# Latent heads in 64 plain and 32 turned rows, a mask laid out beforehand, and eight gate tiles moved into the MLP

## The chip, the core and the metric

The kernel runs on one core of one Trainium2 chip. The metric is the device time of one execution in microseconds, lower is better. A core has five engines with queues of their own: TensorE (PE in the profile; PEld is its weight loads), VectorE (DVE), ScalarE (ACT), GpSimd (POOL) and SyncE (SP), which here only issues transfers. They meet in semaphores.

## What is computed

Two transformer blocks run one after the other on 256 tokens of width 1024, in float32. The first has two layers (a window and neighbourhood attention beside 256 context tokens, then a differential attention), each with an MLP of width 4096. The second has two layers that mix a latent attention (6 heads), a dilated attention (6 heads) and a sparse one (4 heads). What the change touches is this:

```python
# first block: shifts, scales and gates of every layer come from small vectors
mx = jax.nn.silu(c) @ ada_w[i] + ada_b[i]            # 6 x 1024 columns, for x and for ctx
...
s_nb = einsum(q, kb) * scale + bias                  # neighbourhood: bias from b_rpb
s_nb = jnp.where(mask, s_nb, -jnp.inf)               # 16 of the columns of a grid row
...
hx = hx + gx2 * _mlp(...)                            # gx2: the last gate
# second block, latent attention
qa = heads(cq @ w_uq[l], 6)                          # a head: 64 plain + 32 turned
qa_rope = apply_rope(qa[..., 64:], cos, sin)
ka_nope = heads(ckv @ w_uk[l], 6)                    # 64 a head
ka_rope = apply_rope(p_kr, cos, sin)                 # 32, shared by all heads
s = (qa_nope . ka_nope + qa_rope . ka_rope) * 96 ** -0.5   # causal
```

## The kernel before

Feature rows lie on the 128 partitions, tokens in the columns. All weights come as a stream of 286 units of 128 x 1024 float32 (`wall`) through a ring of four slots `raw`. ACT rounds a unit to its high half `whi` (`split_hi`, line 501), DVE subtracts and gets the low half `wlo` (`split_lo`, line 768), and PE multiplies high with high, high with low and low with high (`mm3`, lines 1351 to 1353). Both halves are made three units ahead (`ahead`). A unit gives 128 output features: 24 matmuls, of 512 columns in the first block's first layer, of 256 later. `project`, `values`, `project_out` and `mlp` on PE run over the units. The first three units of each are interleaved (`TOGETHER`).

**Gate tiles.** The adaptive parameters are computed on the side. 144 tiles of 128 x 1024 (`aall`) come through a second ring of four, `aring`. The first 16 are used by PE at the start, eight by PE inside the first attention (`ada_tile`), and the others by DVE as dot products of a row with a broadcast vector: `ada_dot` (line 795) for the first layer's tiles, `ada_dots` (line 826) inside the first MLP. A tile of kind "d" takes two dots (x and context), "s" and "b" one. Where they are used is written out by hand: `ADA_L0` says how many tiles follow each of the 12 steps of the first projection and the 8 steps of the first output projection (`ada_tiles`), `ADA_STEPS` which kinds follow each of the 16 steps of an MLP quarter, four quarters. Biases are added behind (`ada_bias` line 810, `ada_sums` line 838). SP issues weights and tiles in one queue in that same order (`mlp_loads`), each behind a wait that its slot is free.

**Start and first attention.** `project(p_l0)` makes ten query and key units, rotated (`rope`, lines 927 to 930, on DVE; its cosine product on POOL, line 1295), and two value units. POOL adds a column mask from `cst` to the position bias `BI` in two instructions (line 1305, semaphore `rpb_done`), on which DVE waits before the attention. `attend` exists on PE, ACT, DVE and POOL. A job is two heads over up to 256 queries; its scores (line 1484), bias and maxima (952 to 959), exponentials (613), transposes (1501), values (1532), normalisation (1018) and split are spread over seven steps of a software pipeline. PE begins it after `a_used` says that the tiles before it are done. The output projection's results are added to X by DVE (line 1064); squares of ACT are summed by POOL (1234) and PE (1398) for the next norm.

**First MLP.** `mlp` on DVE does in step j: `split_lo` of unit j + 3, then the step's dots, then for j < 8 the square of the ReLU (line 1083) and the low half of the hidden tile (line 1073), for j >= 8 the gated addition to X (line 1064). PE's unit 8 contracts over all eight hidden tiles and waits before its k-th group for the k-th low half (semaphore `hid`). The whole is a loop of four quarters on every engine. The last gate (columns 40 to 47 of `ada`), which the additions use, is computed before the MLP.

**Latent attention, twice.** The query of a head has its own unit, six units (`p_uq`, six k-steps each): rows 0 to 63 plain, 64 to 95 turned. Each is rotated over 96 rows, with a cosine of one on the first 64. ACT copies `w_uk`'s results in six pieces to `KA` (lines 737, 738); POOL copies the turned key, which came in the ninth unit of `p_a` beside the index key, into all six heads (line 1322, `kr_done`), adds the selection to `AL` (line 1326) and only then makes the rotations' cosines. ACT copies the index key twice into `KI`. A score matmul contracts over 96 rows. In `attend` POOL widens the reciprocals (line 1249), then multiplies the row by the gate (line 1256), for which DVE's line 1018 waits, and makes low halves (line 1260).

Of the kernel before, what the change touches and what calls it, by code (L numbers as in the profile page):

```python
# [26 lines left out]
F32 = mybir.dt.float32  # L27
# [25 lines left out]
C_WIN, C_NBR, C_CAU = 1280, 1792, 2304  # L53
C_END = 2688
# [19 lines left out]
B2_UNITS = B2_FM1 + B2_FM2 + 6 + KT + 6 + 1 + 1 + KT  # L74
# [21 lines left out]
def program(nc, wall, aall, const, prm, xin, rpb, ali, out):  # L96
    with ExitStack() as top:
# [85 lines left out]
        QA = sb("QA", [P, 6, N], F32, b2)  # L183
        KA = sb("KA", [P, 6, N], F32, b2)
        VA = sb("VA", [P, 2, 384], F32, b2)
        KK = sb("KK", [P, N], F32, b2)
        KI = sb("KI", [P, N], F32, b2)
# [109 lines left out]

        p_l0 = Proj(U_L0, [l0_tile(i) for i in range(L0_FM)])
# [15 lines left out]
        for l in range(2):  # L314
            u = U_B2 + l * B2_UNITS
            p_a.append(Proj(u, [Tile(256, None, PQ[:, i, :]) for i in range(8)] + [Tile(256, "m", KK[0:96, :])]))
# [7 lines left out]
            p_uq.append(Proj(u + 37, [Tile(256, "m", QA[0:96, i, :], None, 96 ** -0.5) for i in range(6)]))  # L324
# [5 lines left out]
        class Job:  # L330
# [3 lines left out]
            def __init__(self, q, k, parts, bias, v, dst, b0=0, sink=None, diff=False, gate=None, tile=None):  # L334
# [4 lines left out]

        def two(ap, n):  # L340
            return ap[:, None, :].to_broadcast([P, 2, n])

# [74 lines left out]
        def _(sp):  # L417
# [14 lines left out]
            def mlp_loads(u0, ada=False):  # L432
                with sp.Fori(0, QUARTERS) as it:
# [61 lines left out]
        def _(act):  # L495
# [44 lines left out]
            def evac(pr, i):  # L540
# [7 lines left out]
                n = 128 if t.rope == "q" else 96  # L548
                if r >= 2:
                    act.wait_ge(sem("rope_out"), r - 1)  # L550
                ins = act.activation(wk1[0:n, r % 2, 0:N], bank[0:n, 0:N], ACT.Copy, scale=t.scale)
                if t.rest is not None:
                    ins = act.activation(t.rest, bank[:, N:2 * N], ACT.Copy, scale=t.scale)
# [134 lines left out]
            for l in range(2):  # L688
# [41 lines left out]
                for i in range(6):  # L730
# [12 lines left out]
                out_proj(u0 + 45, norms[f"ln{l}"])  # L743
# [1126 lines left out]
```

## Time and profile before

| | |
|---|---|
| runs, median of 3 | 1475.39 us (1473.77 to 1479.74) |
| the profiled execution | 1478.54 us, its span 1476.7 us |
| mean granted clock of TensorE | 0.947 |
| busy: PE, PEld | 1359.0 us (92%), 1177.8 us (80%) |
| busy: DVE, ACT, POOL | 1039.2 us (70%), 643.8 us (44%), 225.9 us (15%) |
| read from memory | 233.90 MB, 159 GB/s over the span |

The span runs from the first to the last instruction. Busy times add up an engine's instructions; a matmul's end is modelled and overlaps the next one's start, so a busy PE is not one at its peak. PE's matmul of 512 columns is shown with 0.39 to 0.40 us and starts about every 0.23 us at full clock. An idle time belongs to the wait that ended it.

### The profile page before, as it was taken

The numbers are of one execution on the slowest core, as the hardware profiler recorded it, in microseconds if no ns is written. First come the engines' busy times: TensorE is split into PE (matmuls) and PEld (weight loads), VectorE is DVE, ScalarE is ACT, GpSimd is POOL, SyncE is SP. The second block draws the span as 40 slices with busy tenths as digits, with TensorE's granted clock in tenths as the row PEclk, the third lists the DMA queues.
The fourth block names the chain that finished last, engine by engine and source line by source line (L and its number), as shares of the span: only waits on it lengthen the run. The fifth ranks groups of instructions, "written<-read, shape, count | busy, mean of one in ns | idle before, by whom it ended". The sixth has DMA issues, their size and how long they took to land. (4 is left out here: it accounts for less than half of the span.)

```text
span 1476.7 us, 24608 instructions
## 1 busy us (share of the span) xinstructions
PE 1359.0 (92%) x9014; PEld 1177.8 (80%) x9014; DVE 1039.2 (70%) x1803; ACT 643.8 (44%) x1287; POOL 225.9 (15%) x294
## 2 busy tenths in 40 slices
PE   6898999499999999979999999999999978899977
PEld 4576678388888888868896789999899967899857
DVE  0698867889697796988416675766664975755964
ACT  2424761242231423325226654455455465455563
POOL 2030221100000000012102710000210126010324
PEclk7898999699999999989999999999999989899988
DMA  7954124357578575744220155665465533445511
GB/s 279 274 172 156 55 62 143 128 185 268 188 243 284 194 264 179 253 175 143 87 90 25 30 157 171 213 185 185 132 222 171 162 96 107 144 144 170 173 42 44
DMA packets 67799, 236.14 MB, mean 160 GB/s; under 512 B 7296, under 2 KB 12416, under 8 KB 67456
## 3 DMA queue, kind: packets, MB, share of 16 engines
q1 hardware_dynamic: 67712, 234.98, 48.7%
q8 instruction: 54, 0.88, 0.2%
q14 instruction: 33, 0.27, 0.1%
HBM read 233.90 MB, written 1.05 MB: 159 GB/s over the span
## 5 line engine op out<-in xcount | busy, mean ns | idle before, releaser
L768 DVE TENSOR_TENSOR wlo<-raw,whi 128x1024 fp32r<-128x1024 f32 x286 | 361.8, 1267 | 176.4 <-ACT whi L501 171.9
L501 ACT ACTIVATE whi<-raw 128x1024 fp32r<-128x1024 f32 x286 | 301.6, 1055 | 244.3 <-PE ps L1353 232.4
L1351 PE MATMUL ps<-Hh,whi 128*128 128x512 f32 (+1 forms) x848 | 297.2, 351 | 17.3 <-DVE Hl L885 14.2
L1352 PE MATMUL ps<-Hl,whi 128*128 128x512 f32 (+1 forms) x848 | 295.1, 348 | 0.0
L1353 PE MATMUL ps<-Hh,wlo 128*128 128x512 f32 (+1 forms) x848 | 295.0, 348 | 0.0
L1351 PEld LDWEIGHTS ps<-Hh,whi 128*128 128x128 f32 x848 | 162.9, 192 | 41.7 <-issue 14.8
L1351 PE MATMUL ps<-Gh,whi 128*128 128x256 f32 x624 | 180.5, 289 | 4.5 <-DVE Gl L885 3.8
L1352 PEld LDWEIGHTS ps<-Hl,whi 128*128 128x128 f32 x848 | 163.1, 192 | 21.4
L1353 PEld LDWEIGHTS ps<-Hh,wlo 128*128 128x128 f32 x848 | 162.7, 192 | 21.8
L1352 PE MATMUL ps<-Gl,whi 128*128 128x256 f32 x624 | 179.0, 287 | 0.0
L1353 PE MATMUL ps<-Gh,wlo 128*128 128x256 f32 x624 | 178.7, 286 | 0.0
L1352 PE MATMUL ps<-HIDl,whi 128*128 128x512 f32 (+1 forms) x512 | 173.2, 338 | 0.0
L1353 PE MATMUL ps<-HIDh,wlo 128*128 128x512 f32 (+1 forms) x512 | 173.2, 338 | 0.0
L1351 PE MATMUL ps<-HIDh,whi 128*128 128x512 f32 (+1 forms) x512 | 173.2, 338 | 0.0
L826 DVE CUSTOM_DVE_ANT_0 ps<-aring,SB 128x1024 f32<-128x1024 f32 x112 | 144.3, 1288 | 3.8 <-DVE AC L826 2.6
L1351 PEld LDWEIGHTS ps<-Gh,whi 128*128 128x128 f32 x624 | 121.8, 195 | 5.9 <-issue 4.7
L1352 PEld LDWEIGHTS ps<-Gl,whi 128*128 128x128 f32 x624 | 121.8, 195 | 0.0
L1353 PEld LDWEIGHTS ps<-Gh,wlo 128*128 128x128 f32 x624 | 121.7, 195 | 0.0
L1351 PEld LDWEIGHTS ps<-HIDh,whi 128*128 128x128 f32 x512 | 96.3, 188 | 11.7
L1353 PEld LDWEIGHTS ps<-HIDh,wlo 128*128 128x128 f32 x512 | 96.3, 188 | 11.7
L1352 PEld LDWEIGHTS ps<-HIDl,whi 128*128 128x128 f32 x512 | 96.3, 188 | 11.5
L613 ACT ACTIVATE wk<-ps,small 128x512 f32<-128x512 f32 (+2 forms) x160 | 84.1, 538 | 21.9 <-issue 10.4
(212 smaller groups left out, 2110.9 us busy)
## 6 DMA issues: line engine op xcount, KB each, us to landing
raw<-wall SPq DMA_DIRECT2D x286, 512.0 KB, 4.3
aring<-aall SPq DMA_DIRECT2D x144, 512.0 KB, 4.4
AL<-ali SPq DMA_DIRECT2D x14, 192.0 KB, 5.4
X<-xin SPq DMA_DIRECT2D x1, 2048.0 KB, 11.7
BI<-rpb SPq DMA_DIRECT2D x4, 512.0 KB, 16.6
cst<-const SPq DMA_DIRECT2D x1, 1216.0 KB, 11.4
out<-X SPq DMA_DIRECT2D x4, 256.0 KB, 2.5
par<-prm SPq DMA_DIRECT2D x1, 134.5 KB, 2.2
```

The costliest lines, as they stand in the source:

```text
L501: act.activation(whi[:, slot, :], raw[:, slot, :], ACT.Copy).then_inc(sem("w_hi"), 1)
L613: ins = act.activation(E[:, s % 2, r, c0:c0 + nk], ps[:, 2 * (s % 2) + r, c0:c0 + nk], ACT.Exp, bias=st[:, x:x + 1], accum_out=st[:, 4 + x ...
L768: dve.tensor_tensor(wlo[:, slot, :], raw[:, slot, :], whi[:, slot, :].bitcast(F32), ALU.subtract)\
L826: ins = dve.tensor_tensor_reduce(ps[:, 6:8, :].rearrange("p b n -> p (b n)"), w, SB[:, v, :], 1.0, 0.0, ALU.mult, ALU.add, AC[:, c:c + 1])
L1351: pe.matmul(o, a[0], b[0], start=first, stop=False)
L1352: pe.matmul(o, a[0], b[1], start=False, stop=False)
L1353: return pe.matmul(o, a[1], b[0], start=False, stop=last)
```

## The change

- Latent queries: the six units become five. Unit 0 holds the turned rows of heads 0 to 3, unit 1 those of heads 4 and 5 (64 rows used), units 2 to 4 the plain rows, two heads each. Only the first two are rotated.
- A score of a latent pair is two plain matmuls of 64 rows and then two of 32 rows for the turned part, added in the same bank. The turned key is made twice in `KK` and shifted into `KX`, so that each head finds it on its own 32 rows; `KX` also serves as the shifted index key. `KA`, POOL's copy and `kr_done` go; `KN` takes three evacuations for six.
- The neighbourhood mask is in `rpb` when it is loaded. POOL's two additions go, `cst` is 512 columns shorter, and DVE waits for the four transfers itself.
- Gate tiles: ten instead of twelve before the attention, six (4, 1, 1) instead of twelve in the output projection, and the last gate's eight ("g", two dots each) in steps 0 to 7 of the MLP's first quarter, which DVE and SP have written out ahead of a loop of three. The other quarters' tiles have a new order. The dots of the first layer's tiles start from the bias instead of 0.0.
- In `attend` POOL multiplies by the gate before it widens the reciprocals.

```diff
 UNITS = U_B2 + 2 * B2_UNITS
...
 ADA_GROUPS = 2
 ADA_EARLY = 2 * KT
-ADA_ROWS = ADA_EARLY + 32
-ADA_L0 = (0, 1, 1, 1, 1, 1, 1, 1, 1, 1, 2, 1, 2, 1, 2, 1, 2, 1, 2, 1)
+ADA_L0 = (0, 1, 1, 1, 1, 1, 1, 1, 1, 1, 1, 0, 4, 1, 1, 0, 0, 0, 0, 0)
 ADA_PROJ = sum(ADA_L0[:12])
 ADA_JOBS = 8
-ADA_STEPS = ("ss", "d", "ss", "d", "ss", "s", "s", "", "d", "bb", "bb", "bb", "bb", "bb", "bb", "d")
-ADA_TURN = "".join(ADA_STEPS)
-ADA_TILES = QUARTERS * len(ADA_TURN)
-ADA_UNITS = ADA_ROWS + ADA_TILES
-AC_D, AC_S, AC_B, AC_END = 0, 8, 16, 28
+ADA_ROWS = ADA_EARLY + 24
+ADA_FIRST = ("g",) * 8 + ("ss", "d") * 4
+ADA_STEPS = ("ss", "d", "bb", "bb") * 4
+ADA_TURN = len("".join(ADA_STEPS))
+ADA_LEAD = ADA_ROWS + len("".join(ADA_FIRST)) - ADA_TURN
+ADA_UNITS = ADA_LEAD + QUARTERS * ADA_TURN
+AC_D, AC_S, AC_B, AC_END = 0, 8, 16, 32
...
-            p_uq.append(Proj(u + 37, [Tile(256, "m", QA[0:96, i, :], None, 96 ** -0.5) for i in range(6)]))
+            p_uq.append(Proj(u + 37, [Tile(256, "r", QR[:, 0, :], None, 96 ** -0.5),
+                                      Tile(256, "h", QR[0:64, 1, :], None, 96 ** -0.5)]
+                             + [Tile(256, None, QN[:, i, :], None, 96 ** -0.5) for i in range(3)]))
...
+        def group(h):
+            return slice(32 * (h % 4), 32 * (h % 4) + 32)
+        def turning_keys(h):
+            return (KX if h % 4 < 2 else KK)[group(h), :]
...
-                    q=(lambda p, r, i=i: QA[0:96, 2 * i + r, P * p:P * p + P]),
-                    k=(lambda p, r, i=i: KA[0:96, 2 * i + r, 0:KLEN[p]]), parts=KLEN,
+                    q=(lambda p, r, i=i: QN[rows(r), i, P * p:P * p + P]),
+                    k=(lambda p, r, i=i: KN[rows(r), i, 0:KLEN[p]]), parts=KLEN,
+                    qr=(lambda p, r, i=i: QR[group(2 * i + r), (2 * i + r) // 4, P * p:P * p + P]),
+                    kr=(lambda p, r, i=i: turning_keys(2 * i + r)[:, 0:KLEN[p]]),
...
-                    a = ADA_ROWS
+                def quarter(it, steps):
+                    a = ADA_LEAD if steps is ADA_STEPS else ADA_ROWS
                     for j in range(16):
                         weight(16 * it + (u0 + j), (u0 + j) % SLOTS)
-                        for _ in ADA_STEPS[j] if ada else ():
-                            ada_unit(len(ADA_TURN) * it + a, a % ADA_SLOTS)
+                        for _ in steps[j]:
+                            ada_unit(ADA_TURN * it + a, a % ADA_SLOTS)
                             a += 1
+
+                if ada:
+                    quarter(0, ADA_FIRST)
+                with sp.Fori(1 if ada else 0, QUARTERS) as it:
+                    quarter(it, ADA_STEPS if ada else ("",) * 16)
 
             sp.dma_start(par[:, :], prm).then_inc(sem("par_landed"), 16)
             sp.dma_start(cst[:, 0:C_COS], const[:, 0:C_COS]).then_inc(sem("cst_landed"), 16)
...
-                for r in range(2):
-                    ins = act.activation(KI[rows(r), :], KK[0:64, :], ACT.Copy)
-                ins.then_inc(sem("ki_shift"), 1)
+                act.activation(KX[0:64, :], KK[64:128, :], ACT.Copy)
+                act.activation(KX[64:128, :], KK[0:64, :], ACT.Copy).then_inc(sem("ki_shift"), 1)
...
+                ahead(u0 + 42)
+                act.wait_ge(sem("w_used"), u0 + 43)
+                for i in range(3):
+                    act.activation(KN[:, i, :], ps[:, (p_uk[l] + i) % 4, 0:N], ACT.Copy).then_inc(sem("proj_out"), 1)
                 ahead(u0 + 43)
-                act.wait_ge(sem("w_used"), u0 + 44)
-                for i in range(3):
-                    bank = ps[:, (p_uk[l] + i) % 4, 0:N]
-                    act.activation(KA[0:64, 2 * i, :], bank[0:64, :], ACT.Copy)
-                    act.activation(KA[0:64, 2 * i + 1, :], bank[64:128, :], ACT.Copy).then_inc(sem("proj_out"), 1)
-                ahead(u0 + 44)
-                evac_v(u0 + 44, V_UV[l], [VA[:, t, :] for t in range(2)])
+                evac_v(u0 + 43, V_UV[l], [VA[:, t, :] for t in range(2)])
...
+                    if kind == "g":
+                        c = 40 + seen
+                        at = [(v, ada[:, v, c:c + 1], par[:, P_AB + c:P_AB + c + 1]) for v in range(2)]
+                    else:
+                        at = [(v, AC[:, c + seen:c + seen + 1], 0.0)
+                              for v, c in {"d": [(0, AC_D), (1, AC_D + 4)], "s": [(0, AC_S)], "b": [(2, AC_B)]}[kind]]
+                    for v, to, start in at:
+                        ins = dve.tensor_tensor_reduce(ps[:, 6:8, :].rearrange("p b n -> p (b n)"), w, SB[:, v, :], 1.0,
...
-            ada_bias(16, 16 + ADA_PROJ)
-            dve.wait_ge(sem("rpb_done"), 1)
+            dve.wait_ge(sem("rpb_landed"), 16 * 4)
             attend(*J_L0)
             add_out(U_L0_OUT, 0, gated(0, 16, 512), 12)
-            ada_bias(16 + ADA_PROJ, 48)
+            ada_bias(16 + ADA_PROJ, 16 + ADA_PROJ + ADA_JOBS)
...
+                    if j0 <= s - 4 < j1 and jobs[s - 4].gate is not None:
+                        g = s - 4
+                        row = RA[:, g % 2, :]
+                        pool.wait_ge(sem("row_out"), HL[g])
+                        pool.tensor_tensor(row, row, jobs[g].gate, ALU.mult).then_inc(sem("row_gated"), 1)
...
-            pool.wait_ge(sem("rpb_landed"), 16 * 4)
-            for t in range(2):
-                ins = pool.tensor_tensor(BI[:, t, :, :], BI[:, t, :, :],
-                                         cst[:, None, C_NBR + N * t:C_NBR + N * t + N].to_broadcast([P, 8, N]), ALU.add)
-            ins.then_inc(sem("rpb_done"), 1)
...
-                pool.wait_ge(sem("rope_out"), p_a[l].r0 + 1)
-                pool.tensor_copy(KA[64:96, :, :], KK[64:96, None, :].to_broadcast([32, 6, N])).then_inc(sem("kr_done"), 1)
-                pool.wait_ge(sem("kr_done"), l + 1)
...
                                 ins = pe.matmul(ps[:, 2 * (s % 2) + r, c0:c0 + nk], j.q(p, r), j.k(p, r),
-                                                start=True, stop=True)
+                                                start=True, stop=j.qr is None)
+                            for r in range(2 if j.qr else 0):
+                                ins = pe.matmul(ps[:, 2 * (s % 2) + r, c0:c0 + nk], j.qr(p, r), j.kr(p, r),
+                                                start=False, stop=True)
...
-                pe.wait_ge(sem("rope_out"), p_uq[l].r0 + 6)
-                pe.wait_ge(sem("kr_done"), l + 1)
+                pe.wait_ge(sem("rope_out"), p_uq[l].r0 + 2)
```

## Rows read from the trace of the kernel before

**Rows 1.** The page, part 1: busy us (share of the span) xinstructions

```profile
PE 1359.0 (92%) x9014; PEld 1177.8 (80%) x9014; DVE 1039.2 (70%) x1803; ACT 643.8 (44%) x1287; POOL 225.9 (15%) x294
```

**Rows 2.** Timeline, 79 to 128 us: start, us, engine, line, operation, [idle before <-releaser]

```profile
79.76 0.42 DVE L928 TENSOR_TENSOR wk<-wk,cst 128x256 f32<-128x256 f32 x1
...
82.35 11.17 POOL L1305 TENSOR_TENSOR BI<-BI,cst 128x2048 f32<-128x2048 f32 x2
...
83.57 5.47 DVE L768 TENSOR_TENSOR wlo<-raw,whi 128x1024 fp32r<-128x1024 f32 x1
...
89.45 4.35 DVE L928 TENSOR_TENSOR wk<-wk,cst 128x256 f32<-128x256 f32 x1
...
98.11 0.50 PE L1351 MATMUL ps<-Hh,whi 128*128 128x512 f32 x1 [3.07 <-DVE wlo L768]
...
99.40 0.63 PE L1353 MATMUL ps<-Hh,wlo 128*128 128x512 f32 x1
...
102.78 0.39 PE L1352 MATMUL ps<-Hl,whi 128*128 128x512 f32 x1
...
122.69 1.21 ACT L560 ACTIVATE V<-ps 128x256 f32<-128x256 f32 x4 [4.63 <-PE ps L1353]
...
127.39 3.79 PE L1484 MATMUL ps<-K,Q 64*128 64x512 f32 x12 [4.73 <-DVE ada L795]
```

**Rows 3.** Timeline, first output projection, DVE and PE

```profile
233.49 0.88 DVE L1064 SCALAR_TENSOR_TENSOR X<-ps,ada,X 128x256 f32<-128x256 f32 x2 [7.31 <-PE ps L1353]
...
277.88 1.84 PE L1398 MATMUL ps<-cst,RS 128*128 128x2 f32 x8 [14.99 <-POOL RS L1234]
...
280.25 0.88 DVE L1064 SCALAR_TENSOR_TENSOR X<-ps,ada,X 128x256 f32<-128x256 f32 x2
```

**Rows 4.** Timeline, first MLP, quarters 0 and 1, DVE and PE

```profile
325.35 1.22 DVE L768 TENSOR_TENSOR wlo<-raw,whi 128x1024 fp32r<-128x1024 f32 x1
...
330.62 1.22 DVE L768 TENSOR_TENSOR wlo<-raw,whi 128x1024 fp32r<-128x1024 f32 x1
...
338.51 1.22 DVE L768 TENSOR_TENSOR wlo<-raw,whi 128x1024 fp32r<-128x1024 f32 x1
...
340.37 0.69 DVE L1073 TENSOR_TENSOR HIDl<-wk,HIDh 128x512 fp32r<-128x512 f32 x1
...
341.28 0.40 PE L1351 MATMUL ps<-HIDh,whi 128*128 128x512 f32 x1
...
430.14 0.69 DVE L1073 TENSOR_TENSOR HIDl<-wk,HIDh 128x512 fp32r<-128x512 f32 x1
```

**Rows 5.** Latent projection and first scores; last, a window's busy times, clock, DMA, GB/s

```profile
1384.64 0.38 ACT L551 ACTIVATE wk<-ps 96x256 f32<-96x256 f32 x1 [0.51 <-PE ps L1353]
...
1386.76 0.38 ACT L551 ACTIVATE wk<-ps 96x256 f32<-96x256 f32 x1 [0.79 <-PE ps L1353]
...
1391.32 0.43 DVE L927 STREAM_SHUFFLE wk<-wk 96x256 f32<-96x256 f32 x1
...
1406.13 4.77 PE L1484 MATMUL ps<-KA,QA 96*128 96x128 f32 x16 [1.54 <-ACT VA L560]
...
1413.05 2.59 PE L1484 MATMUL ps<-KA,QA 96*128 96x128 f32 x8 [2.15 <-ACT wk L613]
...
1416.85 0.93 PE L1484 MATMUL ps<-KQ,QZ 64*128 64x128 f32 x8
...
1406.10:1411.00 4.90, 4.77 (x16) 3.93 (x16) 2.29 (x4) 0.00 (x0) 0.00 (x0) 0.60 0.69 214
```

**Rows 6.** Waits: who <- for whom: us in total, times, longest

```profile
DVE MO L1018 <- POOL RS L1256: 14.9, 16, 1.8
```

**Rows 7.** Timeline, a middle job of the last attention, POOL and DVE

```profile
1426.95 0.40 POOL L1249 COPY RC<-small 128x256 f32<-128x256 f32 x1 [2.54 <-DVE small L978]
...
1427.31 0.73 POOL L1256 TENSOR_TENSOR RS<-RS,GT 128x256 f32<-128x256 f32 x1
...
1428.07 0.42 DVE L1018 TENSOR_TENSOR MO<-ps,RS 128x256 f32<-128x256 f32 x1 [0.74 <-POOL RS L1256]
```

More of the change, by code:

```diff
@@ L315, in program @@
             u = U_B2 + l * B2_UNITS
-            p_a.append(Proj(u, [Tile(256, None, PQ[:, i, :]) for i in range(8)] + [Tile(256, "m", KK[0:96, :])]))
+            p_a.append(Proj(u, [Tile(256, None, PQ[:, i, :]) for i in range(8)] + [Tile(256, "m", KK[64:128, :], KK[0:64, :])]))
             p_b.append(Proj(u + 9, [b2_tile(i) for i in range(B2_FM2)]))
@@ L330, in program, with __init__ @@
         class Job:
-            def __init__(self, q, k, parts, bias, v, dst, b0=0, sink=None, diff=False, gate=None, tile=None):
+            def __init__(self, q, k, parts, bias, v, dst, b0=0, sink=None, diff=False, gate=None, tile=None,
+                         qr=None, kr=None):
                 self.q, self.k, self.bias, self.b0 = q, k, bias, b0
@@ L813, in ada_dots @@
             def ada_dots(it, j):
-                turn = len(ADA_TURN)
-                before = "".join(ADA_STEPS[:j])
-                for n, kind in enumerate(ADA_STEPS[j]):
+                first = isinstance(it, int)
+                steps, lead = (ADA_FIRST, ADA_ROWS) if first else (ADA_STEPS, ADA_LEAD)
+                before = "".join(steps[:j])
+                for n, kind in enumerate(steps[j]):
                     p = len(before) + n
-                    seen = (before + ADA_STEPS[j][:n]).count(kind)
-                    slot = p % ADA_SLOTS
+                    sofar = before + steps[j][:n]
+                    seen = sofar.count(kind)
+                    slot = (lead + p) % ADA_SLOTS
@@ L828, in ada_dots @@
                         if len(at) > 1 and v == 0:
                             ins.then_inc(sem("a_dots"), 1)
-                            dve.wait_ge(sem("a_dots"), 4 * it + (seen + 1))
+                            pairs = sofar.count("g") + sofar.count("d") + 1
+                            dve.wait_ge(sem("a_dots"), 4 * it + ((0 if first else 8) + pairs))
                     ins.then_inc(sem("a_used"), 1)
-                    dve.wait_ge(sem("a_used"), turn * it + (ADA_ROWS + p + 1))
+                    dve.wait_ge(sem("a_used"), ADA_TURN * it + (lead + p + 1))
@@ L1069, in mlp, with quarter @@
             def mlp(u0, h0, T, s, ada=False):
-                with dve.Fori(0, QUARTERS) as it:
+                def quarter(it):
                     def lo(j):
@@ L1092, in mlp @@
                         ada_sums(it)
+                if ada:
+                    quarter(0)
+                with dve.Fori(1 if ada else 0, QUARTERS) as it:
+                    quarter(it)
             dve.memset(scs[:, :, :], 0.0).then_inc(sem("dve_link"), 1)
@@ L1194, in _ @@
                     topk_round(l, i)
-                steps(p_uq[l], 0, 6)
+                steps(p_uq[l], 0, 5)
+                ahead(u0 + 42)
                 ahead(u0 + 43)
-                ahead(u0 + 44)
                 if l == 0:
@@ L1251, in attend @@
                             .then_inc(sem("rc_wide"), 1)
-                    if j0 <= s - 4 < j1 and jobs[s - 4].gate is not None:
-                        g = s - 4
-                        row = RA[:, g % 2, :]
-                        pool.wait_ge(sem("row_out"), HL[g])
-                        pool.tensor_tensor(row, row, jobs[g].gate, ALU.mult).then_inc(sem("row_gated"), 1)
                     if j0 <= s - 5 < j1:
@@ L1697, in _ @@
                 pe.wait_ge(sem("proj_out"), V_UV[l] + 2)
[L1698 to L1699 removed]
+                pe.wait_ge(sem("rope_out"), p_uq[l].r0 + 2)
                 attend(*J_B2[l])
[L1701 removed]
+                project_out(u0 + 44, 16 + 8 * l, 256, Gx, ("o_lo", [HL[J_B2[l][0] + k] for k in range(KT)]))
                 moments(norms[f"ln{l}"], l)
@@ L1777, in ada_stream @@
     later[turned] = w[:, :, 2048:].reshape(KT, P, 32, P).transpose(2, 1, 0, 3).reshape(32, P, 1024)[turned]
-    tiles = np.concatenate([a["ada_w"][1], a["w_ada_2"][0], a["w_ada_2"][1]], axis=1).T.reshape(ADA_TILES, P, 1024)
-    order = []
-    for q in range(QUARTERS):
-        at = {"d": 4 * q, "s": 16 + 8 * q, "b": 48 + 12 * q}
-        for kind in ADA_TURN:
-            order.append(at[kind])
-            at[kind] += 1
-    return np.concatenate([rows, later, tiles[order]])
+    tiles = np.concatenate([a["ada_w"][1], a["w_ada_2"][0], a["w_ada_2"][1]], axis=1).T.reshape(-1, P, 1024)
+    kinds = {"g": later[24:], "d": tiles[0:16], "s": tiles[16:48], "b": tiles[48:]}
+    order = "".join(ADA_FIRST) + 3 * "".join(ADA_STEPS)
+    mlp = [kinds[kind][order[:n].count(kind)] for n, kind in enumerate(order)]
+    return np.concatenate([rows, later[:24], np.stack(mlp)])
 def constants():
@@ L1853 @@
     const, ali = constants()
-    pad = np.zeros((8, 7, 127), np.float32)
-    pad[:, :, 48:79] = a["b_rpb"][0][PAIRS][:, 4:11]
-    rpb = np.stack([pad[:, :, 63 - q:127 - q] for q in range(64)]).reshape(64, 8, 7 * 64)
+    rpb = np.full((64, 8, 7, 64), NEG, np.float32)
+    for q in range(64):
+        k = min(max(q - 8, 0), 48)
+        rpb[q, :, :, k:k + 16] = a["b_rpb"][0][PAIRS][:, 4:11, k - q + 15:k - q + 31]
+    rpb = rpb.reshape(64, 8, 7 * 64)
     arrays = {
```

83 lines of the change are left out of this document (40 added, 43 removed).

## The prediction

> **What bounds the kernel now.** I read the page first: TensorE (PE) is busy for 92% of the span [rows 1], so a removed step is worth time only where PE stands idle. The waits and the timelines then show where it does, and every such place that the change touches is set by VectorE (DVE) or GpSimd (POOL).
>
> In the first projection PE stood idle for 3.07 us at 98.11, waiting for a weight split of DVE. DVE was late because POOL's two additions of the mask ran for 11.17 us from 82.35, and two DVE instructions under them took 5.47 and 4.35 us, where a split takes 1.22 [rows 4] and the other form took 0.42 just before: 8.2 us lost. After the idle time PE's matmuls took 0.63 us instead of 0.39, from 99.40 until shortly before 102.78, the lower of its two clock levels (1.2 instead of 2.4 GHz). The attention then began at 127.39 after 4.73 us of waiting for DVE's last gate tile, though the values had been ready from 122.69 + 1.21 on [rows 2].
>
> In the first output projection DVE works behind PE: PE ended it at 277.88 - 14.99 = 262.89, DVE's last addition ended at 280.25 + 0.88 = 281.13 [rows 3].
>
> In the first MLP PE never stops, but only just. A quarter has 16 units. A matmul of unit 8 needs the last low half of the hidden tiles (line 1073); this ended at 340.37 + 0.69 = 341.06 and PE's first use began at 341.28, in the next quarter 430.83 [rows 4]. From step 1 to step 7 DVE runs without a pause. That is 0.22 us of room, and nobody sees it in a busy share of 70%.
>
> In the latent part of a last-block layer the rotations pass from ACT to POOL to DVE and back, six times; the attention starts at 1406.13 behind the evacuation of VA [rows 5]. Inside that attention DVE stands idle for POOL's gate product (14.9 us over 16 times, [rows 6]), which POOL does only after its 0.40 us copy: 0.74 us of idling in a middle job [rows 7].
>
> **The sum.** It is made against the profiled execution (1478.54, span 1476.7) and its gain is taken off the median 1475.39; the two stand 3.2 us apart, and I take the gain to be the same.
>
> *First projection, and its attention's start.* The mask product on POOL goes (8.2 us of DVE), and two of the twelve tiles before the attention go (a two-dot step takes 330.62 - 325.35 = 5.27, a step without dots 338.51 to 341.06 = 2.55, [rows 4]: 2.7 us a tile, 5.4 us). DVE's last tile comes forward by up to 13.6 us, more than PE can use. PE loses its 3.07 us of idle time and its slow stretch: 8 matmuls some 0.2 us longer, 1.6 us. The values then are ready at 122.69 + 1.21 - 4.7 = 119.2, and the attention starts there instead of 127.39: 8.2 us. It also starts after 1.2 instead of 4.73 us of idling, so its first scores may keep the full clock: 0 to 1.9, I take 0.9. **9.1 us**, bounds 7.5 and 10. The wait on the mask's four transfers passes from POOL to DVE; POOL began the mask at 82.35, so they have landed by then: nothing.
>
> *Output projection.* Six pairs of dots leave it, four of the six left stand in step 0, where DVE waited 7.31 us for PE (the two extra tiles take 5.4). Steps 1 and 2 keep one tile. DVE is back with PE by the fifth unit, so its last addition ends at 262.89 + 0.88 = 263.8 instead of 281.1. PE still sums RS for 1.84 before the last square: **17.1 us**, bounds 15 and 17.5. What is late next is PE's own work.
>
> *MLP, the charge.* Eight tiles of two dots go in. Per quarter steps 0 to 7 had 12 dots (2, 2, 2, 2, 2, 1, 1, 0), now 16. Steps 5 to 7 took 341.06 - 330.62 = 10.44 us and now take 3 x 5.27 = 15.81: the last low half comes 5.37 us later. With 0.22 of room PE stands still for 5.15 us in each of four quarters, 20.6 us. Steps 8 to 15 had two dots each and keep them; there DVE is faster than PE and catches up, so nothing is added. The cover is gone: behind the stall every engine shifts. PE's clock falls, as it did after 3.07 us: 1.6 us each (bounds 0 and 3), 6.4 in all. **27.0 us**, bounds 20 and 34. Transfers: 44 pieces a quarter instead of 40, with the ring of four two steps ahead; hidden. Dots that start from the bias instead of 0.0: the same form but for one operand; between 0 and 0.1 us each, I take 0. Quarter 0 written out: more code, no more work; 0 to 1 us, taken at 0.
>
> *Latent projection, twice.* A unit takes PE 1386.76 - 1384.64 = 2.12 us [rows 5]. POOL's selection addition stays, and holds DVE until 1391.32, so unit 4 ends at about 1393.6 as now. Then: key unit to 1395.9; the value unit needs its split (DVE from 1391.32: rotation 1.8, split 1.2, rotation 1.3, split 1.2, so 1396.8; a rotation is 0.43 and twice 0.42, the first 0.5 longer behind POOL's cosines) and ends at 1398.9; VA's two evacuations of 384 columns take 0.9, since four of 256 took 1.21 [rows 2]. The attention starts at about 1399.9 instead of 1406.13: 6.2 a layer, 12.4 together, bounds 9 and 13. The six evacuations to KA become three, POOL's broadcast copy goes, one evacuation of 0.38 comes; all beside PE's work.
>
> *Scores.* Columns don't shrink. Before, four matmuls in turn stream 128 + 128 + 256 + 256 = 768 columns a job; now plain pairs side by side take 384 and turned pairs side by side 384 more. The gain can only be the clock: jobs 0 and 1 took 4.77, job 2 2.59 at a granted clock near 0.60, while an eight-matmul job at full clock took 0.93 [rows 5]. PE now arrives without the idle stretches before 1406. At full clock 3.3 us a layer would go; with a clock that falls again in the wait for the first exponentials, little. I take 2 a layer, 4, bounds -2 and 6.6. The Trainium skill speaks against this edit: "TensorEngine Tiling (Array Packing)", section Tiling Modes (Key Properties), says that a change of tiling mode drains TensorE, and the new job changes it four times. No row here has a 32-row matmul. The job of 0.93 us is 0.29 above its 384 columns' 0.64, so at most 0.3 a drain is my estimate by that rule: 1.2 us a job, four jobs on the path, the sum 4.8 us smaller, which is inside my range.
>
> *POOL's order.* The gate product is free to run as soon as the row is out, beside DVE's maxima. Four idle stretches of 0.74 a layer go [rows 7] and some of the tail's: 3.6 a layer, 7.2, bounds 3 and 9. Next late is DVE itself, with about 2.9 us of work a job against a period of 3.6.
>
> Together 9.1 + 17.1 + 12.4 + 4 + 7.2 - 27.0 = 22.8 us: **1452.6 us**.
>
> **Rivals.**
> A. The moved dots are hidden in the MLP, as DVE's busy share of 70% suggests. Against it stand the 0.22 us of room and the unbroken chain. It would give 1452.6 - 27.0 = 1425.6.
> B. The scores and POOL's order bring nothing and the clock costs its upper bound: 1452.6 + 11.2 + 5.6 = 1469.4, within 0.5% of before.
> C. Slower: after each stall in the MLP PE stays at the half clock. In the latent attention it did so for some 9 us (1406.13 to 1413.05 + 2.59), in thin work; in dense work the one stretch lasted 3.4 us [rows 2, 5]. A stretch of L us costs L/2. It decides from 18 us on: 1475.4 + 7.4 needs 30.2 more, 7.6 a quarter above the 1.6. At 30 us each the time is 1452.6 + 4 x 13.4 = 1506. Against it: PE works densely behind each stall.
>
> **How the numbers follow.** About 0.5% (7.4 us) is what a measurement of this kernel tells from no change. The forecast has 0.76, its own bounds (ends not all at once) 1440 to 1466; A 0.12; B 0.07; C 0.05. The range 1436 to 1470 takes in B and leaves out A, C and small tails, 2 in 10. Faster than 1468 are the forecast's case, A's and a third of B's, less a small tail: 0.87; same 0.08; slower 0.05.
>
> **What would show it.** In the profile after: no POOL instruction over 5 us near 82 and no 3 us gap at 98; the attention's first scores near 119; additions of the output projection that wait for PE. Then, in every MLP quarter, an idle stretch of about 5 us of PE before unit 8's last matmuls, released by line 1073's successor, and matmuls of 0.63 us behind it; a quarter of about 96.5 us instead of 89.8. If PE shows no such gap, the step on the MLP is wrong. The latent attentions should start 6 us sooner after the projection's first unit, and DVE's period there be near 2.9. If PE is at half clock for much longer than 4 us behind each gap, C holds.

## The result, and the profile after

The changed kernel took 1462.45 us (median of four runs, 1462.23 to 1463.56), the kernel before beside it 1475.55 (1473.77 to 1479.74): a ratio of 0.9913, 95% interval 0.9895 to 0.993. The forecast was 1452.6 in a range of 1436 to 1470: faster, as said, but by 13.1 us of medians where 22.8 were forecast. The two executions with a trace have spans of 1476.7 us before and 1460.4 after, 16.3 apart. The stages below add up to these 16.3, about 3 us more than the medians show.

The page of the kernel after, parts 1 and 5 (in part 5: line, engine, operation, count | busy, mean ns | idle before, releaser):

```profile
span 1460.4 us, 24421 instructions
PE 1358.9 (93%) x9026; PEld 1171.6 (80%) x9026; DVE 1016.7 (70%) x1766; ACT 639.9 (44%) x1279; POOL 204.0 (14%) x282
...
L1379 PE MATMUL ps<-HIDh,whi 128*128 128x512 f32 (+1 forms) x512 | 178.1, 348 | 20.0 <-DVE HIDl L1105 20.0
...
L1380 PE MATMUL ps<-HIDl,whi 128*128 128x512 f32 (+1 forms) x512 | 176.8, 345 | 0.0
```

PE is as busy as in [rows 1], and DVE has 22.5 us less to do. The idle time in front of the HIDh matmuls is new: 20.0 us, released by the successor of line 1073.

I cut both traces at the same steps of the work, by the starts of PE's first matmul in each. Before and after, in us of the profiled span (this table is worked out from the timelines):

```
                                        before             after      difference   forecast
first projection's start            48.44              48.41
first attention starts              127.39             119.18         -8.2         -9.1
output projection starts            217.65             209.27         -0.2
first MLP starts                    289.23             263.21        -17.6        -17.1
next layer's projection starts      661.97             665.23        +29.3        +27.0
latent projection, layer 0         1170.48            1171.50         -2.2          0
its attention starts               1194.56            1189.24         -6.3         -6.2
its output projection              1230.14            1222.22         -2.6         -5.6
latent projection, layer 1         1382.32            1373.38         -1.0          0
its attention starts               1406.13            1391.13         -6.1         -6.2
its output projection              1441.34            1425.29         -1.1         -5.6
end                                1476.7             1460.4          -0.3          0
```

Two parts are off: the latent attentions (the stretches between "its attention starts" and "its output projection") gave 3.7 us for 11.2, and the MLP cost 2.3 more, while the stretches that the change does not touch gave 3.5.

**Where it came as predicted.** The first attention's start (timeline of after, ACT, PE and DVE):

```profile
117.92 1.21 ACT L585 ACTIVATE V<-ps 128x256 f32<-128x256 f32 x4 [4.64 <-PE ps L1381]
...
119.18 0.70 PE L1512 MATMUL ps<-K,Q 64*128 64x512 f32 x2 [1.30 <-ACT V L585]
...
120.43 0.43 DVE L984 TENSOR_TENSOR ps<-ps,cst 128x256 f32<-128x256 f32 x1 [5.40 <-PE ps L1512]
```

The values now release PE, and it is DVE that waits, where in [rows 2] PE waited 4.73 us for DVE. In the output projection DVE stands idle for PE's matmuls, and PE sums without the 14.99 us of [rows 3] (DVE, then PE; RS has no wait before it at all):

```profile
254.56 0.88 DVE L1096 SCALAR_TENSOR_TENSOR X<-ps,ada,X 128x256 f32<-128x256 f32 x2 [3.24 <-PE ps L1381]
...
254.36 0.95 PE L1426 MATMUL ps<-cst,RS 128*128 128x2 f32 x8
256.15 1.54 PE L1426 MATMUL ps<-cst,wk 128*128 128x2 f32 x8 [0.84 <-ACT wk L545]
```

**The MLP.** Its second quarter (PE and DVE in order of time), beside [rows 4]:

```profile
412.01 0.49 PE L1379 MATMUL ps<-HIDh,whi 128*128 128x512 f32 x1 [0.67 <-DVE HIDl L1105]
...
414.33 1.23 DVE L855 CUSTOM_DVE_ANT_0 ps<-aring,SB 128x1024 f32<-128x1024 f32 x1
...
416.16 0.69 DVE L1115 TENSOR_TENSOR wk<-wk 128x512 f32<-128x512 f32 x1 [0.54 <-DVE AC L855]
416.89 0.69 DVE L1105 TENSOR_TENSOR HIDl<-wk,HIDh 128x512 fp32r<-128x512 f32 x1
...
417.64 0.79 PE L1379 MATMUL ps<-HIDh,whi 128*128 128x512 f32 x1 [4.67 <-DVE HIDl L1105]
...
423.35 0.60 PE L1380 MATMUL ps<-HIDl,whi 128*128 128x512 f32 x1
423.77 0.41 PE L1381 MATMUL ps<-HIDh,wlo 128*128 128x512 f32 x1
```

The stall is there in all four quarters: 4.5, 5.3, 5.1 and 5.0 us, 19.9 in all, where I had 20.6. It comes in two pieces, 0.2 to 0.7 us before one group and 4.3 to 4.7 us before the last one, some 5 us later. A quarter takes 98.4 and 97.0 us (second and third) where I had 96.5. From 417.64 to 423.77 PE's matmuls take 0.6 us instead of 0.4, the lower clock. The stretches at the lower clock, counted from the end of the stall, lasted 5.2, 6.1, 3.6 and 5.7 us in the four quarters: they cost half of that, 10.3 us, where I had 6.4.

**The latent attention.** Last layer, PE's scores of the first three jobs and of the fourth (count of records in one merged row, each f32 matmul being two):

```profile
1391.13 0.49 PE L1512 MATMUL ps<-KN,QN 64*128 64x128 f32 x4 [0.96 <-ACT VA L585]
1391.55 0.49 PE L1515 MATMUL ps<-KX,QR 32*128 32x128 f32 x4
1391.97 0.70 PE L1512 MATMUL ps<-KN,QN 64*128 64x256 f32 x4
1392.60 0.70 PE L1515 MATMUL ps<-KX,QR 32*128 32x256 f32 x4
1393.23 0.80 PE L1512 MATMUL ps<-KN,QN 64*128 64x128 f32 x4
...
1395.84 1.22 PE L1515 MATMUL ps<-KK,QR 32*128 32x256 f32 x4
1397.30 0.80 PE L1512 MATMUL ps<-KN,QN 64*128 64x128 f32 x4 [0.23 <-ACT wk L638]
...
1402.53 1.65 PE L1512 MATMUL ps<-KQ,QZ 64*128 64x128 f32 x8
```

A job's scores take 2.1 us at the full clock (1391.13 to 1393.23) and 3.8 at the half (1397.30 to the end of its four groups at 1401.1). Before, two jobs in a row took 4.77 us at a granted clock of 0.60 [rows 5], which is about 1.4 us a job at the full clock. So the new scores are longer, not shorter. Nor is PE at the half clock for less time (the granted clock of a window is the third number from the end; 0.50 is the half clock; after, then before):

```profile
1393.18:1406.83 13.65, 13.41 (x64) 0.50 0.16 63
```

```profile
1403.24:1410.06 6.82, 5.28 (x18) 0.50 0.63 207
1410.06:1413.47 3.41, 1.26 (x7) 1.00 0.03 11
1413.48:1416.88 3.40, 3.40 (x15) 0.50 0.00 0
```

That is 13.7 us in this layer, where before had 10.2 in two pieces, the first from 2.9 us ahead of the attention. Part of the longer scores is hidden: behind them PE waits 0.23 us for ACT's first exponentials, where it waited 2.15 us before [rows 5]. Behind that the middle jobs follow each other on DVE in 2.8 us instead of 3.6, as predicted (2.9). POOL's order did what it should in the middle jobs (waits of after):

```profile
DVE MO L1050 <- POOL RS L1282: 7.8, 8, 1.2
```

against 14.9 us in 16 waits [rows 6]; the 0.74 us of [rows 7] are gone from the middle and the waits that stay are in the tails.

### The profile page after: what moved, and what is told of

It reads as the page before. It is cut to its first block and busy times, and to the rows that moved or that the text cites. A ratio compares the mean times of both kernels' runs of the same rounds, so it can differ in the third digit from the quotient of the medians.

```text
span 1460.4 us, 24421 instructions
## 1 busy us (share of the span) xinstructions
PE 1358.9 (93%) x9026; PEld 1171.6 (80%) x9026; DVE 1016.7 (70%) x1766; ACT 639.9 (44%) x1279; POOL 204.0 (14%) x282
## 5 line engine op out<-in xcount | busy, mean ns | idle before, releaser
L791 DVE TENSOR_TENSOR wlo<-raw,whi 128x1024 fp32r<-128x1024 f32 x284 | 355.6, 1255 | 175.4 <-ACT whi L525 170.1
L1379 PE MATMUL ps<-HIDh,whi 128*128 128x512 f32 (+1 forms) x512 | 178.1, 348 | 20.0 <-DVE HIDl L1105 20.0
L1380 PE MATMUL ps<-HIDl,whi 128*128 128x512 f32 (+1 forms) x512 | 176.8, 345 | 0.0
L1381 PE MATMUL ps<-HIDh,wlo 128*128 128x512 f32 (+1 forms) x512 | 176.3, 344 | 0.0
L1379 PEld LDWEIGHTS ps<-HIDh,whi 128*128 128x128 f32 x512 | 98.7, 193 | 35.6 <-DVE HIDl L1105 23.4
L1381 PEld LDWEIGHTS ps<-HIDh,wlo 128*128 128x128 f32 x512 | 98.6, 193 | 12.4
L638 ACT ACTIVATE wk<-ps,small 128x512 f32<-128x512 f32 (+2 forms) x160 | 84.0, 538 | 17.7 <-issue 8.9
```

Of the source, the lines that this page charges most:

```text
L638: ins = act.activation(E[:, s % 2, r, c0:c0 + nk], ps[:, 2 * (s % 2) + r, c0:c0 + nk], ACT.Exp, bias=st[:, x:x + 1], accum_out=st[:, 4 + x ...
L791: dve.tensor_tensor(wlo[:, slot, :], raw[:, slot, :], whi[:, slot, :].bitcast(F32), ALU.subtract)\
L1379: pe.matmul(o, a[0], b[0], start=first, stop=False)
L1380: pe.matmul(o, a[0], b[1], start=False, stop=False)
L1381: return pe.matmul(o, a[1], b[0], start=False, stop=last)
```

## The experiments

Each kernel is the one after, or the one before, with the edit shown. Gains by stage are differences of the same steps as in the table.

**e1: the dots of the MLP where DVE has time.** The same pieces in another order.

```diff
-ADA_FIRST = ("g",) * 8 + ("ss", "d") * 4
-ADA_STEPS = ("ss", "d", "bb", "bb") * 4
+ADA_FIRST = ("gd", "g", "g", "g", "g", "s", "s", "", "ss", "gs", "d", "gs", "d", "g", "ss", "d")
+ADA_STEPS = ("dddd", "ss", "ss", "ss", "s", "b", "s", "", "bb", "bb", "bb", "bb", "bb", "bb", "bb", "b")
```

> The changed kernel with the 32 dots of each MLP quarter laid out anew: eight in step 0 (quarter 0: four), where the profile of after shows DVE idle for 10.6 us before the first squared tile (quarter 0: 3.05 us), ten or fewer in steps 1 to 7, the rest behind step 8. Same dots, same transfers, same sums. Theory (DVE's low halves in steps 5 to 7 set unit 8): the four stalls of PE (20.0 us) go, and with them the half clock behind them (about 10 us): 1462.5 - 30 = 1432.5, between 1428 and 1437. Rival 1 (the charge is DVE's or the transfers' total load in the MLP, wherever the dots stand): 1455 to 1463. Rival 2 (the half clock comes by itself in the MLP, only the stalls go): about 1442.5.

It took 1427.75 us (1427.64 to 1430.27; ratio to before 0.9668, 0.9636 to 0.97), 34.7 us less than after, 0.3 us below the range that theory gave it (1428 to 1437). The timeline of DVE at the start of the second quarter:

```profile
366.37 1.23 DVE L855 CUSTOM_DVE_ANT_0 ps<-aring,SB 128x1024 f32<-128x1024 f32 x1
...
370.72 0.69 DVE L1115 TENSOR_TENSOR wk<-wk 128x512 f32<-128x512 f32 x1 [3.06 <-ACT wk L651]
```

Eight dots stand where the kernel before had two and then 10.6 us of waiting, and 3 us of it are still left. In this and the later quarters steps 0 to 7 now hold 17 dots, one more than in after, but only nine of them stand in steps 1 to 7. No stall of PE behind HIDl is found in the trace, and a later quarter takes 89.8 us, as in the kernel before. The whole MLP, from first matmul to the next projection, takes 369.8 us (after 402.0, before 372.7): 32.2 of the 34.7 us are there, and most of the rest lies in stretches that the edit does not touch. So the charge was neither DVE's load in the MLP nor the transfers: it was the place of the dots, and not their number before unit 8 either. Rival 1 falls, and so does rival 2, since the half clock went with the stalls.

**e2 and e7: how far the clock falls.** Again the order alone, with 14 dots in steps 0 to 7 (e2) and 15 (e7), in quarter 0 likewise:

```diff
 # e2
-ADA_STEPS = ("ss", "d", "bb", "bb") * 4
+ADA_STEPS = ("ss", "d", "bb", "bb", "ss", "d", "b", "b", "bb", "bbb", "ss", "d", "ssb", "bb", "d", "bb")
 # e7
+ADA_STEPS = ("ss", "d", "bb", "bb", "ss", "d", "bb", "b", "bb", "bb", "ss", "d", "ssb", "bb", "d", "bb")
```

> The changed kernel with 14 instead of 16 dots in steps 0 to 7 of each quarter (one each in steps 6 and 7) and 18 instead of 16 in steps 8 to 15. Two dots of 1.32 us fewer before unit 8: the stall falls from 5.0 to about 2.4 us a quarter, 10.6 us less in all. It prices the clock behind a stall. If the clock falls as far behind 2.4 us as behind 5 us (2.6 us a quarter): 1462.5 - 10.6 = 1452. If its cost goes with the length of the stall: 1447. If the clock does not fall behind so short a stall: 1462.5 - 10.6 - 10.3 = 1441.6.

> The changed kernel with 15 instead of 16 dots in steps 0 to 7 of each quarter, 17 behind. Between e2 (2.6 us of standing still, the clock fell behind one of four stalls) and after (about 5 us, it fell behind all four, for 3.6 to 6.1 us). Expected stall 3.7 to 3.9 us a quarter. If the clock falls behind most of them: stalls 5 us less, half clock about 8 us in all: 1455 to 1458. If behind none: 1446 to 1449.

e2 took 1447.84 us (1445.64 to 1449.77), e7 1454.42 (1451.78 to 1461.24), just under its first case. The execution with the trace took 1445.64 us in e2, 2.2 below the median, and 1461.24 in e7, 6.8 above it: in e7's trace the clock may have fallen more often than it usually does. First and second quarter of e2, then second of e7, PE:

```profile
315.35 0.50 PE L1379 MATMUL ps<-HIDh,whi 128*128 128x512 f32 x1 [1.86 <-DVE HIDl L1105]
...
317.02 0.63 PE L1379 MATMUL ps<-HIDh,whi 128*128 128x512 f32 x1
...
409.53 0.50 PE L1379 MATMUL ps<-HIDh,whi 128*128 128x512 f32 x1 [2.59 <-DVE HIDl L1105]
409.87 0.40 PE L1380 MATMUL ps<-HIDl,whi 128*128 128x512 f32 x1
```

```profile
414.53 0.80 PE L1379 MATMUL ps<-HIDh,whi 128*128 128x512 f32 x1 [2.98 <-DVE HIDl L1105]
415.12 0.63 PE L1380 MATMUL ps<-HIDl,whi 128*128 128x512 f32 x1
...
419.68 0.39 PE L1379 MATMUL ps<-HIDh,whi 128*128 128x512 f32 x1
```

With each dot of 1.32 us more before unit 8 the stall grows by 1.1 and then 1.5 us a quarter: 9.6 us in the four quarters of e2, 13.9 in e7, 19.9 after. The clock does not follow in proportion. Behind e2's stalls of 2.5 to 2.6 us it stayed at the full level three times of three; it fell once, behind the first quarter's, the shortest (1.9 us), for 3.4 us. e7's stalls are 3.0 to 3.7 us, and like those of after they come in two pieces, 0.2 to 0.7 us and, some 4 us later, 2.8 to 3.0. The clock fell at all four, for 17.7 us in all, so 8.9 us lost, nearly what after loses (10.3) with stalls half as long again. e3 and e4 below have the MLP of after, and with its stalls the clock fell at all eight too; their losses come to 9.9 and 8.1 us. e2's time came out above the 1441.6 of its third case, near the second. The one fall costs 1.7 of these 6.2 us. With 18 dots behind step 8 DVE was 5.68 us late at the sums that end the MLP, where after has 2.19 and e1 1.34: another 3.5, which I had not costed.

**e3: two changes of rows a job instead of four.** The plain pairs of both query blocks first, then the turned ones.

```diff
                         for p, (c0, nk) in enumerate(j.parts):
                             for r in range(2):
                                 ins = pe.matmul(ps[:, 2 * (s % 2) + r, c0:c0 + nk], j.q(p, r), j.k(p, r),
-                                                start=True, stop=j.qr is None)
-                            for r in range(2 if j.qr else 0):
+                                                start=p == 0 or j.qr is None, stop=j.qr is None)
+                        for p, (c0, nk) in enumerate(j.parts if j.qr else ()):
+                            for r in range(2):
                                 ins = pe.matmul(ps[:, 2 * (s % 2) + r, c0:c0 + nk], j.qr(p, r), j.kr(p, r),
-                                                start=False, stop=True)
+                                                start=False, stop=p == 1)
```

> The changed kernel with a latent job's scores in the order plain of both query blocks, then turned of both, so that PE passes from 64-row to 32-row matmuls once a job instead of twice (two changes of mode a job instead of four, counting the way back). In the profile of after eight plain and eight turned records take 2.10 us at full clock, where two jobs' worth of plain pairs would take 1.70, and 3.76 at half clock against 3.18. Theory (the surplus is paid at each change of row groups, 0.10 us at full and 0.15 at half clock): a job's scores take 1.9 and 3.5 us, about 1.5 us less in the whole kernel. Rival (the surplus belongs to each 32-row pair, wherever it stands): scores and time as in after, within 0.5 us.

It took 1461.22 us (1459.23 to 1464.25), which the spread does not tell from after. Its last latent attention, PE:

```profile
1392.65 0.93 PE L1512 MATMUL ps<-KN,QN 64*128 64x128 f32 x8 [0.96 <-ACT VA L585]
1393.51 0.92 PE L1516 MATMUL ps<-KX,QR 32*128 32x128 f32 x8
1394.36 0.93 PE L1512 MATMUL ps<-KN,QN 64*128 64x128 f32 x8
1395.22 0.93 PE L1516 MATMUL ps<-KK,QR 32*128 32x128 f32 x8
1398.43 1.47 PE L1512 MATMUL ps<-KN,QN 64*128 64x128 f32 x8 [2.28 <-ACT wk L638]
1399.82 1.65 PE L1516 MATMUL ps<-KX,QR 32*128 32x128 f32 x8
```

A job takes 1.71 us (1392.65 to 1394.36): 0.39 less, twice what I expected. The rows of both kernels follow one pattern. In after, stretches of 128 and 256 columns take 0.42 and 0.63 us from start to start: 128 more columns cost 0.21 us, and 0.21 us is left over in each. Here a stretch of one row count that streams 384 columns side by side takes 0.85, three times 0.21 and again 0.21 more. At the half clock what is left over is 0.31 (stretches of 0.73 and 1.15 us in after). Each stretch pays this, so a job of four pays 0.84 and a job of two 0.42. PE also kept the full clock through the first two jobs. The attentions with their tails are 32.2 us in both layers, where after has 33.0 and 34.2: 2.7 us less. The first projection of the second block gave 2.6 of them back in this run (74.96 us for 72.38, with a stretch at the half clock from 1105.88 that the kernel before has too and after has not).

The other traces show what of this is the clock. after's order of scores was traced in five kernels, ten attentions: six took 32.9 to 33.1 us with at most 10.2 us at the half clock, four took 34.2 or 34.3 with 13.7 us. The order of e3 was traced in three kernels, and all six attentions took 32.1 or 32.2 us with 6.8 us at the half clock. So the shorter scores bring 0.8 us a layer against the better case and 2.0 against the other.

**e4: POOL's old order.** The five lines of the gate product go back behind the widening copy.

> The changed kernel with POOL's old order alone: the gate product behind the widening copy. Theory (the idle stretches of 0.74 us return in four middle jobs of a layer and two more in the tail, all on the path): 4 to 7 us slower, 1467 to 1470. Rival (PE at half clock and the longer scores now set the pace of the first jobs, so that POOL's order only matters in the later ones): 2 to 4 us slower. Rival 2 (the order brought nothing): within 1 us.

It took 1469.38 us (ten runs, 1464.9 to 1471.18), its profiled execution a span of 1462.9. Waits of DVE, e4:

```profile
DVE MO L1050 <- POOL RS L1292: 14.9, 16, 1.8
```

These are [rows 6] to the digit. Its attentions take 35.9 us in both layers: 2.9 and 1.8 more than after, 4.7 in all. The second difference is too small by the clock: this layer was at the half clock for 13.7 us in after and for 10.2 in e4, and with 10.2 us the same code took 32.9 and 33.0 in it (e2, e9). At like clock POOL's order is worth 2.9 us a layer, 5.8 in all, of the 7.2 that I had. The medians are 6.9 apart, but the stretches outside differ too. The same numbers price the scores: with POOL's old order the new scores give 35.9 twice, the old ones gave 35.6 and 35.2. They cost 1.0 us together, if anything: the old code took anything from 34.0 to 36.2 us in the traces of before, e5 and e6.

**e5: the mask alone,** on the kernel before: the host writes the bias with the mask in it, POOL's additions and their semaphore go.

```diff
-            dve.wait_ge(sem("rpb_done"), 1)
+            dve.wait_ge(sem("rpb_landed"), 16 * 4)
...
-            pool.wait_ge(sem("rpb_landed"), 16 * 4)
-            for t in range(2):
-                ins = pool.tensor_tensor(BI[:, t, :, :], BI[:, t, :, :],
-                                         cst[:, None, C_NBR + N * t:C_NBR + N * t + N].to_broadcast([P, 8, N]), ALU.add)
-            ins.then_inc(sem("rpb_done"), 1)
...
```

> The kernel before with the mask laid out in the bias by the host and POOL's two additions gone; DVE waits for the four transfers. Nothing else. Theory (POOL's 11.17 us held DVE's two instructions under them, 8.2 us lost, and DVE's last gate tile set the attention's start): the last tile comes 8.2 us forward, to where the values are ready, and the first scores start near 119.2 instead of 127.39: about 1467.3, and the two tiles taken out of the first projection in the change bought nothing more. Rival (the idle time at 98 comes from the number of tiles, the mask's additions lie beside other work): 0 to 3 us.

It took 1467.10 us (1466.72 to 1467.79), ratio 0.9945 (0.9928 to 0.9963). Its first attention, ACT and PE:

```profile
117.71 1.21 ACT L560 ACTIVATE V<-ps 128x256 f32<-128x256 f32 x4 [4.64 <-PE ps L1348]
...
119.10 0.70 PE L1479 MATMUL ps<-K,Q 64*128 64x512 f32 x2 [1.43 <-DVE ada L795]
```

The start came to 119.10, after's 119.18 without its two tiles fewer. The mask alone brings the whole gain of this part. The two tiles taken from before the attention bought nothing beside it, and their four dots are among the sixteen that the MLP was given.

**e6: shorter dots in the output projection,** on the kernel before; half of each of these 24 sums is left out.

```diff
+                n = 512 if a >= ADA_PROJ + ADA_JOBS else 1024
                 for v in range(2):
-                    ins = dve.tensor_tensor_reduce(ps[:, 4:6, :].rearrange("p b n -> p (b n)"), aring[:, u % ADA_SLOTS, :],
-                                                   SB[:, v, :], 1.0, 0.0, ALU.mult, ALU.add,
+                    ins = dve.tensor_tensor_reduce(ps[:, 4:6, :].rearrange("p b n -> p (b n)")[:, 0:n],
+                                                   aring[:, u % ADA_SLOTS, 0:n],
+                                                   SB[:, v, 0:n], 1.0, 0.0, ALU.mult, ALU.add,
```

> The kernel before with the 24 dots of the twelve tiles of the output projection over 512 instead of 1024 columns: half of each of these sums is left out. About 0.6 us less a dot, 14 us in all. Theory (DVE's dots alone hold PE at 277.88, as in my term of 17.1 us): the idle time of 14.99 us shrinks to about 1, the time to 1461.5. Rival (POOL's root sums, named as the releaser in that row, hold it): the idle time stays above 10 us, the time within 3 us of before.

It took 1463.91 us (1463.36 to 1468.81). PE at the end of the output projection, and one of the shortened dots:

```profile
269.65 1.84 PE L1400 MATMUL ps<-cst,RS 128*128 128x2 f32 x8 [5.43 <-POOL RS L1236]
```

```profile
264.00 0.70 DVE L796 CUSTOM_DVE_ANT_0 ps<-aring,SB 128x512 f32<-128x512 f32 x1
```

A dot lasts 0.70 instead of 1.23, so 24 of them give 12.7 us, a little less than my 14. From the projection's start to the next part's it is 10.6 us shorter (60.95 us against 71.58); the other 2.1 went into DVE's own wait for PE in front, 9.45 us for the 7.31 of [rows 3]. PE's idle time before its sums fell from 14.99 to 5.43, where I had expected about 1: the dots gave 12.7 us for 14, 2.1 went into that wait, and 1.1 came off only behind these sums. The releaser in that row is POOL, but shorter dots on DVE alone bring it forward: it stands behind DVE. The mechanism of the 17.1 us holds, and the rival falls.

**e8, e9 and e10: the two improvements together.** e8 has the edits of e1 and e3.

> e1 and e3 together: the dots of the MLP early, and a latent job's scores with two changes of rows instead of four. Theory (each stretch of one row count costs 0.21 us on top of its columns at full clock, 0.31 at half, so two stretches fewer a job save 0.4 to 0.6 on three jobs a layer, and PE keeps its full clock longer): 2 to 3 us below e1, 1424.5 to 1426. Rival (PE waits for the first exponentials the longer): as e1, 1427.5.

It took 1428.42 us (1423.85 to 1429.62), e1's time and not the 1424.5 to 1426 of the theory. Its attentions were 32.2 and 32.1 us, 2.8 less than e1's 33.0 and 34.2; a half-clock stretch behind 1073.77 that e1 does not have gave 2.5 back. Both kernels ran again side by side, five times each:

> The kernel of e1 again, beside the one of e8 on the same chip, since their medians (1427.75 and 1428.42, four runs each) lie within the spread of their runs, while the latent attentions of e8's profile were 2.8 us shorter together. Both theories: 1426 to 1429.

> The kernel of e8 again. If the 2.8 us of its latent attentions reach the end (and the slower stretch behind 1021 in e8's profile, 74.86 us to the indexer's weights instead of 72.30, comes and goes with PE's clock in any kernel): 2 to 3 us below e9. If the extra wait for the first exponentials, or that slower stretch, belongs to this version: within 1 us of e9.

e9 took 1427.91 us (1425.69 to 1432.61), e10 1426.98 (1424.45 to 1431.4), with profiled spans of 1425.9 and 1422.5: 3.4 us apart in the traces and 0.9 in the medians, inside the spread of either. Of the 3.4 us the latent attentions hold only 1.5, since e9's took 33.0 us in both layers; the rest lies elsewhere. Both beat the kernel before by 3.2% (ratios 0.9677 and 0.9676). By the stages the shorter scores should bring 1.5 us or more; the times do not settle whether they reach the end.

## Why the prediction was right, and where it was off

*First projection and the attention's start* (9.1): the right mechanism and nearly the size; e5 shows it alone. 8.2 came by the start and 0.2 in the attention, so the 0.9 for the clock of the first scores was too much. That the two tiles lay in excess ("more than PE can use") e5 confirms: they could have stayed.

*Output projection* (17.1): 17.6 measured, the mechanism shown by e6.

*MLP* (27.0): 29.3 measured. The step held: a busy share of 70% hides nothing when a chain without pause ends 0.22 us ahead of its use. The stalls were 19.9 of 20.6; e2 and e7 shorten them by the dots that they take out of steps 6 and 7, and e1 removes them with more dots before unit 8 than after has, but eight of these in step 0, in front of the chain. The mis-sized term is the clock: 4 x 1.6 came from the one stretch of 3.4 us behind 3.07 us of idle time, and the four stretches behind 5 us lasted 3.6 to 6.1, 2.6 us lost each. It was inside the bound of 3. Rival A (hidden in the MLP) fell; what it claimed is true of e1's layout only. Rival C (PE stays at the half clock for 18 us or more) fell at once. Its 9 us in the latent attention were a misreading: the granted clock was full from 1410.06 to 1413.47 in between.

*Latent projection* (12.4): 6.3 and 6.1, as worked out.

*Scores* (4) is the step that failed: they cost about 1 us. The step said that the columns do not shrink, 768 before and after, and that the clock could only give. It left out of the sum that the row which it quoted, 0.93 for 384 columns, shows a fixed part, and that a job now has four stretches with it and had one. At the full clock a job's 768 columns are 1.28 us plus four times 0.21, 2.1, and would be about 1.5 in one stretch. The 1.4 us worked out above for the kernel before agree with that, and its 2.4 and 2.6 us a job were partly at the full clock. At the half clock the new job took 3.8. Nor did PE keep its clock: it fell two microseconds into the attention. The change of row counts I had priced, at most 0.3 us, as a bound alone and not in the sum, where the rows now give 0.21 at the full clock and 0.31 at the half for each stretch. The Trainium skill, "TensorEngine Tiling (Array Packing)", section Tiling Modes (Key Properties), says that a change of tiling mode drains TensorE; the traces of after and of e3 agree that each such stretch is paid for, and the sum by that rule, 4.8 us smaller, would have been the nearer one.

*POOL's order* (7.2): 5.8 by e4 at like clock, 4.7 in the two traces as they are. The right mechanism, a little too large: DVE's waits for POOL fell by 7.1 us (14.9 to 7.8), as counted, but only 5.8 of them came out at the end, and where the other 1.3 went is not shown. In the last layer, the one with the longer half clock, DVE's waits for PE's plain score matmuls (line 984 for line 1512) rose from 0.5 us in e4 to 1.9 in after; in layer 0 they are 0.4 in both. That the two latent attentions together gave only 3.7 of 11.2 us is then the scores (about 5 us off), POOL's order (1.4) and this longer half clock (1.1). Whether the old scores of 96 rows would be quicker in the new order was not tried, since the new layout holds no such rows; that they would be is an estimate from the 1.4 us a job above.

*The rest*: 3.5 us came where nothing was changed. Most of it goes with stretches at the half clock that the profiled execution of before had (5.9 us behind 1052.35 and 3.2 behind 1106.41, after has 3.1 behind 1055.31 and none later) and of which e3, e5, e6, e7 and e8 show the second too, while e1, e2, e4, e9 and e10 do not. Such stretches come and go between executions, and the profiled one of before was 3 us above its median: this part is probably no gain of the change, but no run separates it. By rival B's terms (scores and POOL's order nothing, clock at its upper bound) the time would have been 1469.4; the truth lies between it and the forecast.

## What to carry to other kernels

Before work moves to an engine that is "only 70% busy", find the chain on that engine that another engine waits for, and its room; then look in the same loop for the step where the engine stands idle, and put the work there. The change as made paid some 30 us for dots that cost nothing when eight of them stood in step 0. When a matmul is split into two with fewer rows each, count the stretches of each row count and not the columns alone, and group all matmuls of one row count together; here that was worth 0.4 us a job, too little to show in the whole time.

## What the runs showed of the hardware

A stretch of 64-row or 32-row matmuls costs 0.21 us above its columns at the full clock and 0.31 at the half, and what counts is the number of stretches (after and e3). Pairs in different row groups do run together: 768 columns streamed in 0.85 us. In dense work PE's granted clock did not fall behind three idle stretches of 2.5 to 2.6 us, but fell behind one of 1.9 (e2). It fell at all four of 2.8 to 3.0 us (e7, each with a shorter one some 4 us ahead) and at all twelve of 4.3 to 4.7 us (after, e3, e4). So no length that is safe can be read from these runs. Once it had fallen the loss hardly grew with the stall: 8.9 us in e7 against 10.3, 9.9 and 8.1 us behind the longer stalls of after, e3 and e4. The dot that starts from a bias operand instead of 0.0 takes 1.29 us instead of 1.23, inside the 0 to 0.1 that I had allowed.
